# The first stage of a diffusion-transformer step in another order: filter spectra, modulation and first norm of the tokens

## What is computed

```
mod = silu(c) @ w_ada + b_ada                 # 1024 x 6144, for two condition vectors
h   = rmsnorm(x) * (1 + scale1) + shift1      # the input of the big projection
# filters of the long convolution, for L = 1024 (latent) and L = 256 (context):
h = sin(fr * (emb @ w1 + b1)); h = sin(fr * (h @ w2 + b2))
h = (h @ w3).reshape(L, 2, HYENA_ORDER, D_HYENA) * decay
two_sided = [fwd[0] + bwd[0], fwd[1:], 0, reversed bwd[1:]]
return rfft(two_sided)
```

## Time and profile before

| | |
|---|---|
| median of 3 runs | 2788.02 us (2787.21 to 2791.22) |
| the profiled execution | 2791.18 us, its span 2789.3 us |
| first matmul of the second stage | 225.63 us after the span's start |
| TensorE, busy share of the span | 96% |
| first stage, data moved | 47.13 MB, mean 209 GB/s |

### The profile page before, as it was taken

The page is one execution under the profiler, slowest core; times in us unless marked ns, Lnnn a source line. Parts: engine busy times, 40 slices in busy tenths (PEclk is TensorE's granted clock), DMA queues, the critical chain, the costliest instruction groups (busy, mean ns, idle before and its releaser), DMA issues. The chain is left out here.

```text
span 2789.3 us, 36190 instructions
## 1 busy us (share of the span) xinstructions
PE 2686.1 (96%) x14803; PEld 2312.8 (83%) x14803; DVE 1273.1 (46%) x1853; ACT 896.0 (32%) x1512; POOL 827.7 (30%) x552
## 2 busy tenths in 40 slices
PE   9788999989999999999999799999999999999998
PEld 7567888878888888898887688887888888888887
DVE  6667765545655454445677611435221211212216
ACT  2343221045555455545311521224112121121122
POOL 3546995211001010100244133314233233232230
PEclk9779999999999999999999899999999999999999
DMA  6666776442122312320669422301111111111102
GB/s 205 224 204 233 245 238 212 155 159 97 67 86 92 112 59 96 109 82 34 234 218 324 147 91 87 129 30 42 41 40 38 38 38 38 38 38 38 39 31 76
DMA packets 99027, 314.27 MB, mean 113 GB/s; under 512 B 12065, under 2 KB 29571, under 8 KB 98478
## 3 DMA queue, kind: packets, MB, share of 16 engines
q1 hardware_dynamic: 75726, 231.73, 24.3%
q0 software_dynamic: 23136, 80.22, 8.6%
HBM read 232.75 MB, written 70.78 MB: 109 GB/s over the span
## 5 line engine op out<-in xcount | busy, mean ns | idle before, releaser
L2490 DVE SCALAR_TENSOR_TENSOR tl_x<-tl_b,all_mod,tl_x 128x512 f32<-128x512 f32 (+1 forms) x216 | 142.7, 662 | 351.2 <-PE tl_b L91 348.2
L89 PE MATMUL at_out<-h_hi,hd_nexthi 128*128 128x424 f32 (+1 forms) x672 | 264.6, 394 | 6.7 <-PEq L77 3.4
L89 PE MATMUL tl_b<-tl_hi,tl_whi 128*128 128x512 f32 (+1 forms) x720 | 255.9, 355 | 1.2 <-ACT tl_r L2325 1.2
L90 PE MATMUL tl_b<-tl_lo,tl_whi 128*128 128x512 f32 (+1 forms) x720 | 255.4, 355 | 0.0
L91 PE MATMUL tl_b<-tl_hi,tl_wlo 128*128 128x512 f32 (+1 forms) x720 | 255.0, 354 | 0.0
L540 POOL TENSOR_TENSOR hd_nextlo<-at_raw,hd_nexthi 128x1024 fp32r<-128x1024 f32 x26 | 61.4, 2360 | 628.9 <-ACT hd_nexthi L640 628.9
L722 DVE TENSOR_REDUCE at_nmax<-at_s 128x1 f32<-128x1280 f32 (+1 forms) x160 | 196.9, 1273 | 105.0 <-PE at_s L591 104.3
L90 PE MATMUL at_out<-h_lo,hd_nexthi 128*128 128x424 f32 (+1 forms) x672 | 239.8, 357 | 0.0
L91 PE MATMUL at_out<-h_hi,hd_nextlo 128*128 128x424 f32 (+1 forms) x672 | 239.7, 357 | 0.0
L675 ACT ACTIVATE at_e<-at_s,at_nmax 128x1280 f32<-128x1280 f32 (+1 forms) x160 | 185.3, 1159 | 135.8 <-DVE at_nmax L722 135.8
L2580 DVE TENSOR_TENSOR tl_r<-tl_r 128x512 f32<-128x512 f32 (+1 forms) x96 | 65.7, 686 | 356.3 <-ACT tl_r L2325 356.3
(11 more groups left out here) (340 smaller groups left out, 6383.0 us busy)
## 6 DMA issues: line engine op xcount, KB each, us to landing
hy_tab<-in_hy_tab POOLq DMA_DIRECT2D x68, 512.0 KB, 5.5
mg_nextraw<-in_w_tail SPq DMA_DIRECT2D x36, 512.0 KB, 3.7
tl_raw<-in_w_tail SPq DMA_DIRECT2D x36, 512.0 KB, 3.6
hd_wa<-in_w_adaT SPq DMA_DIRECT2D x32, 512.0 KB, 4.4
at_raw<-in_w_proj SPq DMA_DIRECT2D x26, 512.0 KB, 4.6
fd_in<-in_xT SPq DMA_DIRECT2D x16, 640.0 KB, 4.5
s_gatesT<-at_pad SPq DMA_DIRECT2D x16, 640.0 KB, 2.9
mg_gate<-s_gatesT SPq DMA_DIRECT2D x16, 640.0 KB, 5.0
```

The lines of the kernel that those rows point to most:

```text
L89: pe.matmul(out, w_hi, x_hi, start=first, stop=False)
L90: pe.matmul(out, w_hi, x_lo, start=False, stop=False)
L2490: dve.scalar_tensor_tensor(out=x1[:, n, at:at + m], in0=bank[x % GEMM_BANKS][:, 0:m], scalar=g.mod[:, gate, SEG_OF[c]:SEG_OF[c] + 1], in1= ...
```

## The change

`stage_head` is written anew; what it computes is the same. `stage_heads` only gets other addresses for its tiles. In `stage_head`:

- **Modulation**: `ada(b)` for eight blocks of 256 outputs. Now `silu` is stationary (two columns) and the weights move: eight fp32 matmuls of 256 columns a block into two rows of a bank. ScalarE copies the rows out (`ada_out`), and two small matmuls (`ada_turned`) turn them.
- **Network**: ScalarE does the first of the six operations on the argument (`pre`), GpSimd the sum and difference of `w3` and its lower part.
- **Norm**: all eight squared rows go through `token_sum` (80 matmuls, 50 before); VectorE's `sum_up` is gone. The sums stand between the taps of order 0.
- **Order of TensorE**: taps and context units of order 0 are interleaved with modulation and sums. The pairs of order 1 (`PAIR_ORDER`) are the last of that part and then lie between the latent units of order 0, and four buffers `eo` in place of two hold them.
- **Order of the units**: the four latent units that need only odd tiles come first, so that the pairs of order 1 can be split into tiles that are free again; the even tiles are split in the first units of order 1.
- **Lower parts**: those of the latent tiles of order 0 on VectorE (`first_lows` there, 17 subtractions), the others on GpSimd.
- **Queues**: all stores by SP, from five buffers; GpSimd's queue only loads tables. The second load of the rows goes to buffers of its own (`x_row`), two after each of the last four units of order 0, once all pairs are made.

```diff
+PAIR_ORDER = [(0, 0), (0, 1), (0, 2), (0, 3), (0, 4), (1, 1), (1, 0), (1, 2), (1, 3), (1, 4)]
+PAIR_HOME = [1, 0, 1, 0, 1, 0, 2, 3, 1, 2]
...
+            for i in range(STREAM + 3, len(ITEMS)):
+                load(i)
+            for x in range(2 * R):
+                if RUNS_OF[x % R][1] == "odd":
+                    evacuated(sp, x + 1)
+                else:
+                    evacuated(sp, x)
+                for dst, src in stores(x):
+                    sp.dma_start(dst, src).then_inc(stored[x % OB], 16)
+                if x < R and x + 1 in ROWS_AFTER:
+                    sp.wait_ge(made, len(PAIR_ORDER))
+                    for k in range(2 * ROWS_AFTER.index(x + 1), 2 * ROWS_AFTER.index(x + 1) + 2):
+                        sp.dma_start(x_row[k][:], g.d["xT"][k]).then_inc(row_in[k], 16)
+                if x == R + ODD_DONE:
+                    sp.wait_ge(spec_mm, R + ODD_DONE)
+                    for j in range(2):
                         sp.dma_start(w_raw[j][:], g.d["w_proj"][j * Q_U]).then_inc(w_in, 16)
...
+            first_lows(0)
+            for u in range(CTX_UNITS):
+                next_table(u)
+            for u in range(CTX_UNITS, M):
+                next_table(u)
+                if u == CTX_UNITS + 1:
+                    for i in range(CTX_AT, ODD_AT):
+                        lower(i, low1_ctx)
+                if ODD_UNITS <= u < ODD_UNITS + 4:
+                    at = ODD_AT + 2 * (u - ODD_UNITS)
+                    for i in range(at, at + 2):
+                        lower(i, low1_odd)
...
+            def ada(b):
+
+                if b:
+                    pe.wait_ge(ada_row, b)
+                for q in range(2):
+                    i = 2 * b + q
+                    pe.wait_ge(*landed(ADA_AT[i]))
+                    w = stream[ADA_AT[i] % STREAM][:, 0:D].rearrange("p (k c) -> p k c", k=ADA_K)
+                    for k in range(ADA_K):
+                        mm = pe.matmul(p_ada, g.silu[:, ADA_K * q + k], w[:, k], start=(q == 0 and k == 0),
+                                       stop=(q == 1 and k == ADA_K - 1))
                     mm.then_inc(ada_mm, 1)
-                ada_at[0] += count
-
-            def taps_of(o, p):
-
-                k = o * PAIRS + p
-                if k:
-                    pe.wait_ge(mixed, k)
+
+            def ada_turned(b):
+
+                pe.wait_ge(ada_row, b + 1)
+                for j in range(ADA_N // P):
+                    mm = pe.matmul(pm[:, ADA_N // P * b + j], row_buf[:, j * P:(j + 1) * P], g.ident[0:2, 0:2], start=True,
+                                   stop=True)
+                mm.then_inc(ada_turn, 1)
...
+            pe.wait_ge(done, 1)
             for i in range(NET):
+                ada(i)
                 layer(1, i)
-                modulation(1)
-            modulation(ADA_FIRST - 1 - NET)
-            for o in range(2):
-                for p in range(PAIRS if o == 0 else 0):
-                    k = o * PAIRS + p
-                    if k == 0:
-                        pe.wait_ge(done, 6)
-                    if o == 0:
-                        pe.wait_ge(fs, 2 * (1 + (p + 1) // 2))
-                    taps_of(o, p)
-                    modulation(ADA_BY_PAIR[k])
...
+                ada_turned(i)
+            ada(3)
+            pe.wait_ge(done, 3)
+            pe.wait_ge(w3_l, 1)
+            taps_of(0)
+            ada_turned(3)
+            token_sum(0)
+            ada(4)
+            taps_of(1)
+            unit(0)
+            unit(1)
+            ada_turned(4)
+            token_sum(1)
+            ada(5)
+            taps_of(2)
+            unit(2)
+            unit(3)
+            ada_turned(5)
+            token_sum(2)
+            ada(6)
+            taps_of(3)
+            unit(4)
+            ada_turned(6)
+            token_sum(3)
+            ada(7)
+            taps_of(4)
+            ada_turned(7)
+            token_sum(4)
+            token_sum(5)
+            taps_of(5)
+            token_sum(6)
+            token_sum(7)
+            for u, s in ((CTX_UNITS, None), (CTX_UNITS + 1, 6), (CTX_UNITS + 2, 7), (CTX_UNITS + 3, None), (ODD_UNITS, 8),
+                         (ODD_UNITS + 1, None), (ODD_UNITS + 2, 9), (ODD_UNITS + 3, None)):
+                if s is not None:
+                    taps_of(s)
+                unit(u)
...
+            act.wait_ge(w3_sum, 2)
+            act.activation(w3_hi[:], w3[:], ACT.Copy).then_inc(w3_h, 1)
+            sine(0, 1)
+            pre(1, 0)
+            ada_out(0)
+            sine(0, 2)
...
-            def sum_up(k):
-                dve.wait_ge(squared, k + 1)
-                sq = stream[(X_AT + k) % STREAM]
-                if k == 0:
-                    dve.tensor_copy(acc[:], sq[:]).then_inc(summed, 1)
-                else:
-                    dve.wait_ge(summed, k)
-                    dve.tensor_tensor(acc[:], acc[:], sq[:], ALU.add).then_inc(summed, 1)
...
+            pair(1)
+            for p in LATENT[1:]:
+                pair(p)
+                first_lows(p - 1)
+            first_lows(PAIRS - 1)
+            pair(5)
+            cross(CTX_UNITS)
+            pair(6)
+            cross(CTX_UNITS + 1)
+            pair(7)
+            cross(CTX_UNITS + 2)
+            cross(CTX_UNITS + 3)
+            pair(8)
+            cross(ODD_UNITS + 1)
+            dve.wait_ge(token_sums, KD)
+            dve.wait_ge(ada_turn, ADA_BLOCKS)
+            dve.wait_ge(late_in, 16 * 7)
+            modulations()
+            dve.tensor_reduce(tot[:], p_sum.rearrange("p k t -> p t k"), AX.X, ALU.add).then_inc(tot_done, 1)
+            dve.wait_ge(tot_done, 1)
+            dve.tensor_scalar(var[:], tot[:], 1.0 / D, EPS, ALU.mult, ALU.add).then_inc(var_done, 1)
+            pair(9)
...
+            multiply(1)
+            for i in range(4):
+                cross(M + CTX_UNITS + i)
+                multiply(2 + i)
+            cross(M + ODD_UNITS + 1)
+            multiply(6)
+            lower(0)
+            cross(M + ODD_UNITS + 2)
+            multiply(7)
+            lower(2)
+            cross(M + ODD_UNITS + 3)
+            lower(4)
+            cross(M + ODD_UNITS + 4)
+            lower(6)
+            lower(7)
```

More of the change, by code:

```diff
@@ L814, in filter_units @@
     low = [j for j in range(LAT_FT) if j % 2 == 0 and j < LAT_FT // 2 or LAT_FT // 2 <= j < 3 * LAT_FT // 4]
-    return ctx + [(LAT_FT, 2), (1, 2)] + [(j, c) for j in low for c in range(2)]
+    odd, even = ([j for j in low if even_tile(j) == e] for e in (False, True))
+    return (ctx + [(LAT_FT, 2)] + [(j, c) for j in odd for c in range(2)] + [(1, 2)]
+            + [(j, c) for j in even for c in range(2)])
 def filter_runs():
@@ new lines, in ada_turned, with token_sum @@
+            def ada_turned(b):
[4 more added lines that the diff above has]
+                mm.then_inc(ada_turn, 1)
+            def token_sum(k):
+                pe.wait_ge(squared, k + 1)
+                x = stream[X_AT[k] % STREAM]
+                for tt in range(TT):
+                    mm = pe.matmul(p_sum[:, k, tt:tt + 1], x[:, tt * P:(tt + 1) * P], g.ones[:, 0:1], start=True, stop=True)
+                mm.then_inc(token_sums, 1)
@@ new lines, in _ @@
+            pe.wait_ge(rstd_done, 1)
+            pe.transpose(p_rows, rstd[:], g.ident[:]).then_inc(rows_mm, 1)
+            unit(ODD_UNITS + 4)
+            pe.wait_ge(rows_done, 1)
+            pe.wait_ge(late_in, 16 * 7)
+            pe.wait_ge(mixed, len(PAIR_ORDER))
+            for c, (at, m) in enumerate(CHUNKS):
+                for tt in range(at // P, (at + m) // P):
+                    mm = pe.matmul(spread_bank[c][:, tt * P - at:tt * P - at + P], pick[:, tt], rows[:], start=True,
+                                   stop=True)
@@ L1220, in _, with pre @@
+            mm.then_inc(spread, 1)
+            for u in range(M):
+                unit(M + u)
         @block.scalar
         def _(act):
-            def split(o, p):
-                k = o * PAIRS + p
-                act.wait_ge(made, k + 1)
-                for i, x in enumerate(slots(p)):
-                    act.activation(hi_of(x), eo[k % 2][:, i], ACT.Copy).then_inc(split_hi, 1)
+            def pre(n, i):
+                at, m = NET_CH[i]
+                act.wait_ge(net_mm, n * NET + i + 1)
+                act.activation(y[:, at:at + m], bank[i][:, 0:m], ACT.Identity, bias=fb[:, n:n + 1], scale=vec[:, 2:3]
+                               ).then_inc(net_pre, 1)
@@ new lines, in _ @@
+            pre(0, 0)
+            pre(0, 1)
+            sine(0, 0)
+            pre(0, 2)
+            act.wait_ge(w3_sum, 2)
[4 more added lines that the diff above has]
+            sine(0, 2)
+            pre(1, 1)
+            sine(1, 0)
+            net_out(0)
+            ada_out(1)
+            pre(1, 2)
+            sine(1, 1)
+            net_out(1)
+            sine(1, 2)
+            net_out(2)
```

629 lines of the change are left out of this document (313 added, 316 removed).

## The result

The changed kernel takes 2812.35 us (median of 4, 2808.09 to 2816.29), the kernel before 2787.64 (4 runs, 2787.21 to 2791.22): a ratio of 1.0085, 95% interval 1.0072 to 1.0097. It is slower, by 24.7 us; the forecast was 2773, a gain.

The account below looks back on a forecast made before the run. No engine bounded the whole: chains between engines did, then TensorE's clock. Terms +10.2 + 14.2 - 37.4 - 2.6 = -15.6 us, applied to 2788.0, gave 2772.4, say 2773; range 2750 to 2800.

Parts of the forecast that it names:

- A: Start to first taps, with network and four modulation blocks: first taps at 43 us, +10.2, bounds 39 and 52.
- B: First taps to first latent unit, with taps, blocks, sums and context units at mixed clock: 71 us, +14.2.
- Rival 1: TensorE's clock stays at 2.4 GHz: B is 53, A 39, 22 us less, 2751; chance 0.15.
- rival 2: TensorE's clock stays low in B: A 52, B 95, 33 us more, 2806, slower; chance 0.18.
- C: Latent units of order 0 to the spread's end: 43 us against 80.4, -37.4, bounds 38 and 52.
- the 50 that the prediction itself had named: Sign of error for latent units of order 0 to the spread's end: prediction wrong if C takes over 50.
- D: Spread's end to the second stage's first matmul, units of order 1: 53 us, -2.6, bounds 46 and 60.
- Landings of stores under 4 us: Sign named for the first stage's stores, all sent by SP: they land in under 4 us.
- Row loads in the queue: In C, row loads wait in SP's queue for the last pair, later stores behind them: cost 1 us, within 43.
- Rival 3: Stores land behind row loads, GpSimd in VectorE's way: C 50, D 60, 14 more, 2787; chance 0.16.
- The move to VectorE is free: In B, 17 subtractions, 11.7 us, go to VectorE with 30 us to spare; at most 11.7 if uncovered.
- The 15 that I had worked out: In D, loss by VectorE and GpSimd excluding one another: 15 us by the skill's rule, 8 taken from rows.

Follow-up runs that it names:

- split_all: Changed kernel with all six 127-row stores each sent as 112 and 15 rows; 2773.98 us, ratio 0.9942 to the kernel before.
- rows_act: Changed kernel with the eight row loads moved from SP's queue to ScalarE's, 127-row stores kept whole; 2817.13 us, ratio 1.0103.
- split_rows_late: split_all with loads of token rows 4 to 7 moved behind stores 4 and 6 of order 1; 2776.89 us, ratio 0.9954.
- split_lows_pool: split_all with the 17 latent lower parts of order 0 moved back from VectorE to GpSimd; 2777.91 us, ratio 0.9953.

## Why the prediction was wrong, by its own steps

- **A, first taps at 43** (+10.2): right, at 43.58. Blocks 0 to 3 took 5.90, 3.61, 5.05 and 5.70 us, and TensorE stood 5.29 us for the third sine, forecast 5.
- **B, 71 us**: 62.2. The mechanism was right, its clock too pessimistic: the granted clock was 0.85, the upper end of the forecast range. Three of the four blocks took 3.62 us and five of the eight sums 2.39. The first latent unit came at 105.5, forecast 114. Rival 1 (53) had the direction, rival 2 (95) was wrong.
- **C, 43 us**: 50.2, undersized by 7; inside its bounds (38 and 52), but past the 50 that the prediction itself had named as a sign of being wrong. TensorE was busy for 40.4, where the sum had 30 in it; which wait makes up the rest was not tested. B's surplus of 8.8 hides it: 157 forecast for the spread's end, 156.0 measured, is two errors that cancel, and so luck. The narrow stores have no part in it, since split_all has 50.5 too: 43 was too low by itself.
- **D, 53 us: this step failed**, at 93.5. In it, and in C, I let all stores go over SP's queue at the price of "2.2 us to landing" of the earlier trace rows. The row is right for 128 rows. I carried it over to six stores of 127 rows, of which the trace of before had none on that queue; its own line for them, 254 KB from GpSimd's queue, I did not bring in, nor did I ask what differed. For a price that no row showed, the sum had no term and the range no bound. The runs put 40 us on it (split_all against the changed kernel). With that term my sum is 2773 + 40 = 2813, measured 2812; that it comes so close is luck too, since B and C were off by 8.8 and 7 in opposite directions. "Landings of stores under 4 us", a sign that the prediction had named, failed here, and the second stage began at 249.5 where 210 was named.
- **Row loads in the queue, "I cost it at 1"**: nothing speaks against it: taking them out gained nothing (rows_act), nor did moving half of them with the narrow stores split (split_rows_late). What went unseen is the other direction: the narrow stores held the loads, 14.1 us to landing against 9.1 in split_all. **Rival 3** had store landings late behind row loads and D at 60: the right place, the wrong cause, and with 7 us a fifth of the size.
- **The move to VectorE is free**: right within the noise, some 3 us (split_lows_pool).
- **D's list without the narrow stores**: 56.0 for 53. GpSimd in VectorE's way costs about what was put in for it: in split_all a lower part took 4.85 us beside the weight subtractions and 1.67 alone, and three multiplications 3.48, 2.59 and 3.02 in place of 1.67, together 7.3 us, and 9.4 with two multiplications beside the even lower parts (5.33 in place of 3.26), against the 8 assumed. The 15 that I had worked out from the rule of exclusion in the Trainium skill ("SBUF — State Buffer", Who interferes with whom) would have been too much.
- **GpSimd ends 6 us after the last unit, no later than VectorE**: GpSimd ended at 226.6, 6 us after TensorE (220.7), and no engine's wait names it.

## What to carry to other kernels

When stores or loads move to another queue, list them by shape, not by bytes: the price of the queue holds for the shapes that it carried in the trace. A DMA share of 1/16 with everything idle is one engine at work; from a queue like SP's send a number of rows that is a multiple of 16, and the rest apart (112 and 15 rows landed in under 3 us each, 127 rows took some 10). And when a trace shows waits for a buffer, follow them to the store before blaming the engine named: here TensorE's waits read as ScalarE's and VectorE's.

## What the runs showed of the hardware that was not expected

- One row decides: 128 rows landed in 2.2 us in the kernel before, 127 took some 10 from the same queue, and 4.1 to 4.4 from GpSimd's.
- A narrow store also slows what others move over its engine, and is slowed by it: SP's queue fell from 25 GB/s to 7 beside ScalarE's loads (rows_act).
- TensorE's clock again does not follow the profile's busy time. Windows of the changed kernel, a block of the modulation with 256 moving columns, a token sum behind it, and two sums in a row:

```profile
71.60:75.20 3.60, 3.60 (x19) 1.33 (x18) 2.55 (x5) 1.58 (x4) 0.00 (x0) 1.00 0.89 278
78.80:81.10 2.30, 2.30 (x21) 2.29 (x20) 2.27 (x4) 0.28 (x1) 0.56 (x1) 1.00 0.48 126
...
97.00:105.60 8.60, 8.60 (x43) 8.60 (x41) 6.65 (x12) 0.00 (x0) 0.00 (x0) 0.50 0.00 0
```

TensorE is busy throughout in all three. The block has a stationary operand of two columns and stands at 2.4 GHz; a single sum with one moving column keeps it; the two sums one after the other run at 1.2 GHz, 4.3 us each in place of 2.39, and the first latent unit behind them starts at the slow pace too. The clock had fallen before these two: the sum at 86.8 us still took 2.39 us, TensorE then waited for 0.66, and the next sum took 4.33 and the taps behind it came at the slow pace, 0.43 us apart. Whether the wait or the second sum brought it down was not tested.
